# An encoder trunk on one core: the attention's first loads, the decays' sums and the experts' weight splits at other places

## What is computed

```python
h = rmsnorm(x, g_mix)
q, k, v, z, xbc, dtf, dtb, ga, gs = split(h @ w_in)
ya = windowed_gqa(q, k, v, sink, bias) @ w_attn_out
ys = ssd_branch(z, xbc, dtf, dtb, ...) @ w_ssd_out
x = x + (sigmoid(ga) * ya + sigmoid(gs) * ys) @ w_out
x = x + hier_moe(rmsnorm(x, g_ffn), router_g, router_e, w_gate_up, w_down)
x = x + sigmoid(rmsnorm(x, g_ple) @ w_ple_gate) * (p @ w_ple_proj)
return rmsnorm(x, g_final)
```

## Time and profile before

| what | us |
|---|---|
| three runs | 1834.16, 1846.12, 1836.23 |
| median | 1836.23 |
| the profiled execution, by the device | 1842.91 |
| its span, first to last instruction | 1840.8 |
| PE busy in the span | 1726.6 |

### The profile page before, as it was taken

How to read it: one execution, slowest core, us unless ns; L and a number is a source line. 1 busy time by engine, 2 the same in 40 slices (tenths; PEclk the granted TensorE clock), 3 DMA queues, 4 the chain that set the end, 5 groups by cost and what they waited for, 6 DMA issues and landing times. The chain is left out here.

```text
span 1840.8 us, 27069 instructions
## 1 busy us (share of the span) xinstructions
PE 1726.6 (94%) x10450; PEld 1417.9 (77%) x10451; DVE 885.6 (48%) x1027; ACT 597.5 (32%) x1010; POOL 414.3 (23%) x278
## 2 busy tenths in 40 slices
PE   6999999899999989999999999997999987998897
PEld 5878888787877757777888888885788876785786
DVE  5201777202034127742688425323757886940674
ACT  4311222231111126643455324112534433442332
POOL 3011111111111101002100022000356556652330
PEclk8999999999999999999899999998999998998899
DMA  5211222323355322017675344224767775742452
GB/s 196 86 63 58 78 77 77 110 75 112 129 180 186 89 72 64 27 41 223 221 193 155 127 139 149 80 70 164 259 213 275 282 296 199 282 176 105 163 194 92
DMA packets 115836, 265.90 MB, mean 144 GB/s; under 512 B 13011, under 2 KB 59555, under 8 KB 115740
## 3 DMA queue, kind: packets, MB, share of 16 engines
q1 hardware_dynamic: 99484, 209.11, 34.8%
q0 software_dynamic: 8320, 30.43, 4.9%
q10 hardware_dynamic: 7936, 25.01, 3.8%
HBM read 192.95 MB, written 71.55 MB: 144 GB/s over the span
## 5 line engine op out<-in xcount | busy, mean ns | idle before, releaser
L2139 DVE TENSOR_TENSOR ex_wlo<-ex_raw,ex_whi 128x1024 fp32r<-128x1024 f32 x102 | 166.8, 1649 | 6.9 <-ACT ex_whi L2133 6.9
L2135 DVE CAST ex_whi<-ex_raw 128x1024 fp32r<-128x1024 f32 x96 | 95.2, 997 | 71.0 <-DMA ex_raw<-experts 67.4
L2716 PE MATMUL rt_p<-ex_whi,ex_xh 128*128 x280 | 115.6, 413 | 14.1 <-issue 7.5
L286 PE MATMUL rest_p<-hi_h,whi_in 128*128 128x512 f32 (+1 forms) x480 | 121.9, 362 | 0.0
L286 PE MATMUL rest_p<-lo_h,whi_in 128*128 128x512 f32 (+1 forms) x480 | 119.9, 358 | 0.0
L286 PE MATMUL rest_p<-hi_h,wlo_in 128*128 128x512 f32 (+1 forms) x480 | 119.6, 357 | 0.0
L2717 PE MATMUL rt_p<-ex_wlo,ex_xh 128*128 x280 | 111.3, 397 | 0.0
L2718 PE MATMUL rt_p<-ex_whi,ex_xl 128*128 x280 | 111.3, 397 | 0.0
L889 ACT ACTIVATE rest_out<-rest_p 128x1024 f32<-128x1024 f32 x20 | 20.5, 1025 | 248.0 <-PE rest_p L286 248.0
L286 PEld LDWEIGHTS rest_p<-hi_h,whi_in 128*128 128x128 f32 x480 | 80.1, 188 | 22.1 <-issue 8.2
L920 POOL TENSOR_TENSOR wlo_in<-wraw_in,whi_in 128x1024 fp32r<-128x1024 f32 x18 | 43.8, 2434 | 230.5 <-ACT whi_in L883 230.5
(11 more groups left out here) (393 smaller groups left out, 4072.0 us busy)
## 6 DMA issues: line engine op xcount, KB each, us to landing
ex_raw<-experts SPq DMA_DIRECT2D x96, 512.0 KB, 6.1
wraw_in<-units SPq DMA_DIRECT2D x36, 512.0 KB, 4.4
y_slots<-ex_y ACTq DMA_DIRECT2D x35, 512.0 KB
rest<-rest_out SPq DMA_DIRECT2D x20, 640.0 KB, 6.0
scan_e<-erow SPq DMA_DIRECT2D x32, 256.0 KB
xtok<-conv_tok SPq DMA_DIRECT2D x10, 640.0 KB, 3.3
z_x<-x SPq DMA_DIRECT2D x10, 512.0 KB, 4.0
ao_gate<-rest SPq DMA_DIRECT2D x8, 640.0 KB, 5.1
```

The source lines that it names most:

```text
L286: mm = pe.matmul(out[:, n, 0:size], w[:, kk, :], h[:, kk, c:c + size], start=(kk == 0 and w is whi and h is hi), stop=(kk == ktiles - 1 an ...
L2135: eng.tensor_copy(self.hi[:, e % 2, n, :], self.raw[e % 2][:, n, :]).then_inc(self.w_hi[n], 1)
L2139: eng.tensor_tensor(self.lo[:, e % 2, n, :], self.raw[e % 2][:, n, :], self.hi[:, e % 2, n, :].bitcast(F32), ALU.subtract).then_inc(self.w ...
L2716: pe.matmul(gu[s][:, :], xh[s][:, kk, :], hi, start=(kk == 0), stop=False)
```

## The change

Three edits.

1. The loads of the first two query blocks and key windows, of V and of the sink move from the attention into the stage in front. A new class `Windows` holds these tiles and their semaphores. In the projection SP loads the sink before its loop and, at c = 18, waits for the states' last store, for earlier stores, for the stores of tiles 0 to 5 and for POOL's memset of the key windows, then issues the five loads ahead of store 18; at the stage's end it waits for them. The memset stands at the end of POOL's stream in that stage. The attention keeps the loads for n from 2, has no warm-up, and doesn't wait for V, the sink or the first windows.
2. In PE's order of the projection, product 1 comes ahead of the sums, and the rows' groups follow products 2 and 3; the bias line stands right behind the third group.
3. In the experts DVE does hi(n), lo(n), and then waits for its own low part before the next unit.

```diff
--- before.py
+++ after.py
@@ -815,7 +815,32 @@
         dve.memset(bias[:, 2, :, 2 * P:], NEG)
-def stage_project_rest(k, ctx, block, hi, lo, q, ring, xt_stored, ch_stored, early_copied, early_stored, first_lo, tok_copied):
+class Windows:
+    def __init__(self, k):
+        self.k, o = k, O_R2 + 9 * 4096
+        self.q = k.at("q_blk", [P, 2, 4, P], F32, o)
+        self.k_win = k.at("k_win", [P, 2, BAND], F32, o + 4096)
+        self.v = k.at("v_ch", [P, T], F32, O_W + 6 * 4096)
+        self.sink = k.at("sink", [P, N_HEADS], F32, O_KEEP + 2304)
+        self.qk_in = k.sems(None, "qk_in0", "qk_in1")
+        self.v_in, self.k_zero, self.sink_in = k.sems(None, "att_v_in", "att_k_zero", "att_sink_in")
+    def table(self, n):
+        return 1 if n in (0, QB) else 2 if n in (QB - 1, NT - 1) else 0
+    def load(self, sp, n):
+        s, rest = n % 2, self.k.d["rest"]
+        sp.dma_start(self.q[:, s, :, :], rest[0:4 * P, n * P:(n + 1) * P].rearrange("(m p) t -> p m t", p=P)
+                     ).then_inc(self.qk_in[s], 16)
+        a = 1 if self.table(n) == 1 else 0
+        b = 2 if self.table(n) == 2 else 3
+        sp.dma_start(self.k_win[:, s, a * P:b * P], rest[4 * P:5 * P, (n - 1 + a) * P:(n - 1 + b) * P]
+                     ).then_inc(self.qk_in[s], 16)
+def stage_project_rest(k, ctx, block, hi, lo, q, win, ring, xt_stored, ch_stored, early_copied, early_stored, first_lo, tok_copied):
     nc, d = k.nc, k.d
@@ -856,6 +881,7 @@
                 load(2 + s, s)
             decays.sync(sp)
             tables.sync_tables(sp)
+            sp.dma_start(win.sink[:, :], d["sink"].partition_broadcast(P)).then_inc(win.sink_in, 16)
             for c in range(n_tiles):
                 if c + 4 < n_tiles:
                     load(c + 4, c % 2)
@@ -867,9 +893,23 @@
                     states.load(sp, 1)
                 if FIRST <= c < FIRST + states.STEPS - 2:
                     states.load(sp, c - FIRST + 2)
+                if c == n_tiles - 2:
+                    states.wait_stored(sp)
+                    sp.wait_ge(early_stored, 16 * EARLY)
+                    for s in range(2):
+                        sp.wait_ge(xt_stored[s], 96)
+                        sp.wait_ge(stored[s], 48)
+                    sp.wait_ge(win.k_zero, 1)
+                    for n in range(2):
+                        win.load(sp, n)
+                    sp.dma_start(win.v[:, :], d["rest"][5 * P:6 * P, :]).then_inc(win.v_in, 16)
                 store(c, c % 2)
             for s in range(2):
                 sp.wait_ge(stored[s], 16 * (n_tiles // 2 + 1))
+                sp.wait_ge(win.qk_in[s], 32)
+            sp.wait_ge(win.v_in, 16)
+            sp.wait_ge(win.sink_in, 16)
         @block.scalar
         def _(act):
@@ -927,6 +967,8 @@
             with pool.Fori(3, n_tiles // 2) as i:
                 for s in range(2):
                     rest(2 * i + s, s)
+            states.wait_stored(pool)
+            pool.memset(win.k_win[:, :, :], 0.0).then_inc(win.k_zero, 1)
         @block.vector
         def _(dve):
@@ -957,14 +999,14 @@
                                 wlo[:, s, :].rearrange("p (k c) -> p k c", k=KT), hi, lo, KT).then_inc(mm_done, 1)
             product(0, 0)
+            product(1, 1)
             pe.wait_ge(tok_copied, 33)
             decays.tensor(pe)
-            product(1, 1)
+            product(2, 0)
             decays.tensor_rows(pe, 0)
             decays.tensor_rows(pe, 1)
-            product(2, 0)
+            product(3, 1)
             decays.tensor_rows(pe, 2)
-            product(3, 1)
             tables.tensor_line(pe)
             product(4, 0)
             product(5, 1)
@@ -1204,7 +1246,7 @@
-def stage_attention(k, ctx, block, att_hi, att_lo, ring):
+def stage_attention(k, ctx, block, att_hi, att_lo, ring, win):
@@ -1214,13 +1256,11 @@
     UNITS = 2 * NT
     if True:
         o = O_R1 + 10 * 4096
...
         vn = k.at("v_tok", [P, NT + 4, N_KV, HEAD + 1], F32, o + 12288)
         pt = k.at("probs_t", [P, 4, BAND], F32, o + 19616)
...
         @block.sync
         def _(sp):
-            sp.wait_ge(v_zero, 1)
-            for n in range(NT):
-                s = n % 2
-                if n >= 2:
-                    sp.wait_ge(score_done, 2 * n - 2)
-                sp.dma_start(qs[:, s, :, :], d["rest"][0:4 * P, n * P:(n + 1) * P].rearrange("(m p) t -> p m t", p=P)
-                             ).then_inc(qk_in[s], 16)
-                a = 1 if table(n) == 1 else 0
-                b = 2 if table(n) == 2 else 3
-                sp.dma_start(ks[:, s, a * P:b * P], d["rest"][4 * P:5 * P, (n - 1 + a) * P:(n - 1 + b) * P]
-                             ).then_inc(qk_in[s], 16)
+            for n in range(2, NT):
+                sp.wait_ge(score_done, 2 * n - 2)
+                win.load(sp, n)
                 if n == 3:
                     for u in range(2):
                         sp.dma_start(next_raw[:, u, :], d["units"][U_AO + u]).then_inc(next_in, 16)
         @block.gpsimd
         def _(pool):
-            pool.memset(ks[:, :, :], 0.0).then_inc(v_zero, 1)
             pool.memset(vn[:, :, :, :], 0.0).then_inc(v_zero, 1)
-            pool.wait_ge(v_zero, 2)
+            pool.wait_ge(v_zero, 1)
             pool.memset(vn[:, :, :, HEAD:HEAD + 1], 1.0).then_inc(ones_set, 1)
             for s in range(2):
                 pool.wait_ge(next_in, 32)
@@ -1287,8 +1313,8 @@
         def _(pe):
             def score(u):
                 n, h, s = u // 2, u % 2, u // 2 % 2
-                if h == 0:
-                    pe.wait_ge(qk_in[s], 32 * (n // 2) + 32)
+                if h == 0 and n >= 2:
+                    pe.wait_ge(qk_in[s], 32 * (n // 2))
                 if u:
                     pe.wait_ge(scored, u)
@@ -1328,9 +1354,7 @@
                     mm = pe.transpose(ap_[:, m, :], att[:, n % 2, m * P:(m + 1) * P], ident)
                 mm.then_inc(att_turned, 1)
-            warm_up(pe, k, pv_bank[:, :], 6)
             score(0)
-            pe.wait_ge(v_in, 16)
             for t in range(NT):
                 if t >= 2:
@@ -1359,8 +1383,6 @@
         @block.scalar
         def _(act):
-            act.dma_start(vt[:, :], d["rest"][5 * P:6 * P, :]).then_inc(v_in, 16)
-            act.dma_start(sink[:, :], d["sink"].partition_broadcast(P)).then_inc(sink_in, 16)
             act.preload_act_table(ACT.Exp)
             def exp(u, i):
@@ -1400,7 +1422,6 @@
         @block.vector
         def _(dve):
-            dve.wait_ge(sink_in, 16)
             dve.tensor_scalar(nsink[:, :], sink[:, :], -1.0, None, ALU.mult).then_inc(sink_neg, 1)
             dve.wait_ge(sink_neg, 1)
@@ -2649,15 +2670,15 @@
         def _(dve):
             dve.wait_ge(pp_done, NT)
             for e in range(1, N_EXP + 1):
-                ew.split_hi(dve, e, 0)
                 for n in range(6):
-                    if e == 1 and n == 3:
+                    if e == 1 and n == 4:
                         for s in range(2):
                             dve.wait_ge(pp_stored[s], 16 * (NT // 2))
-                    if n < 5:
-                        ew.split_hi(dve, e, n + 1)
+                    ew.split_hi(dve, e, n)
                     ew.split_lo(dve, e, n)
+                    dve.wait_ge(w_lo[n], e + 1)
         @block.gpsimd
         def _(pool):
...
```

More of the change, by code:

```diff
@@ L1216, in stage_attention @@
         o = O_R1 + 10 * 4096
-        qs = k.at("q_blk", [P, 2, 4, P], F32, o)
-        ks = k.at("k_win", [P, 2, BAND], F32, o + 4096)
-        vt = k.at("v_ch", [P, T], F32, o + 7168)
+        qs, ks, vt, sink, table = win.q, win.k_win, win.v, win.sink, win.table
+        win.qk_in = qk_in = k.sems(ctx, "att_qk_in0", "att_qk_in1")
         vn = k.at("v_tok", [P, NT + 4, N_KV, HEAD + 1], F32, o + 12288)
@@ L1222, in stage_attention @@
         att = k.at("att_tok", [P, 2, N_HEADS * HEAD], F32, o + 25760)
-        sink = k.at("sink", [P, N_HEADS], F32, o + 29856)
         nsink = k.at("nsink", [P, N_HEADS], F32, o + 29888)
@@ L1232, in stage_attention @@
         ap_ = ctx.enter_context(nc.psum_tensor("att_t", [P, 4, P], F32))
-        qk_in = k.sems(ctx, "qk_in0", "qk_in1")
-        names = ("v_in", "v_zero", "v_turned", "v_copied", "sink_in", "sink_neg", "score_done", "scored", "step",
+        names = ("v_zero", "v_turned", "v_copied", "sink_neg", "score_done", "scored", "step",
                  "probs", "turned", "pt_ready", "pv_done", "att_done", "att_turned", "att_hi_s",
                  "att_lo_s", "ready", "pv_step", "ones_set", "sunk")
-        (v_in, v_zero, v_turned, v_copied, sink_in, sink_neg, score_done, scored, step, probs,
+        (v_zero, v_turned, v_copied, sink_neg, score_done, scored, step, probs,
          turned, pt_ready, pv_done, att_done, att_turned, att_hi_s, att_lo_s, ready, pv_step, ones_set, sunk) = k.sems(
@@ L3046, in build @@
         q = SsdTiles(k)
+        win = Windows(k)
         with ExitStack() as ctx:
-            stage_project_rest(k, ctx, block, hi, lo, q, ring, *done)
```

(3 more changed lines are left out.)

2 lines of the change are left out of this document (removed).

## The result

The changed kernel takes 1824.59 us in the median of 13 runs (1820.5 to 1833.59), the kernel before, in 13 runs beside them, 1840.76 (1834.03 to 1848.44). The ratio is 0.9918, 95% interval 0.9899 to 0.9937: 0.8% faster. The forecast was 1824.5 and the range 1816 to 1834, but the agreement is closer than the single steps deserve: part of it is luck, as the sections behind show.

A forecast was written before the change was run, and what follows sets the result against it. PE bounds the kernel, busy 94% of 1840.8 us. Terms 4.5 + 3.6 + 11.5 = 19.6 take 1842.9 to 1823.3; the lowest timed run gives 1826.1; predicted the middle, 1824.5, range 1816 to 1834.

The forecast's parts named there:

- the accident: Experts, profiled execution: POOL's product for hidden values took 11.31 us, shut out by DVE's unbroken splits; PE waited 8.87.
- one of the signs of being wrong: Experts: the prediction is wrong if PE's waits for the low parts rise well above 4.1 us.
- First attention loads: Attention's start: early loads, no filler, score(0) right after the barrier; gain 4.5 us, bounds −2 to 8.1.
- rival 1: Attention without filler stays at half clock through its first units; its gain becomes 0 or −1, total 1829.5 us; chance 0.15.
- Sums a product later: Projection: PE's 5.04 us wait on DVE's decays goes, gain 6.8, less 3.2 exposed; net 3.6 us (1.6 to 4.4).
- The new wait: Projection: line product behind the third rows group waits 2.4 us for ACT's six copies; 0.8 more charged for the clock.
- Splits one by one: Experts: waits between DVE's splits let POOL in; net gain 11.5 us (−21 to 13).
- rival 2: Experts: POOL isn't let in, waits too short or its stall needs another cause; 1834.8 us; chance 0.13.
- the cover: Experts: DVE's 67.4 us idle for late weights hides the added 21.1 us (96 units × 0.22).
- rival 3: Experts: DVE becomes the bound; if none of its added 21.1 us is hidden, 1844.4 us; chance 0.05.
- The level: Whole kernel: timed runs some 11 us apart, as if one of three had the accident; the middle, 1824.5 us, predicted.

The follow-up runs named there:

- the old order and the wait: Changed kernel with hi(n+1) again issued ahead of lo(n), DVE's wait on its own low part kept behind each unit; ratio to the kernel before 0.9894.
- the gap behind every third unit: Changed kernel with hi(n+1) issued ahead of lo(n), DVE's wait on its own low part only behind every third unit; ratio to the kernel before 0.9912.

## Why the prediction was right, and where it was not

The waits and the filler that were to go went, and the sum came near (19.6 forecast against the profiled execution, 17.55 measured). But the three terms were mis-sized and their errors cancel in part, the reason that I gave for the accident is only part of it, and one of the signs of being wrong that I had named came: PE's waits for low parts rose well above 4.1 us.

**First attention loads.** The working by steps held: loads issued before store 18, score(0) at half clock, the softmax of unit 0 not late. I allowed 4.3 or 5.8 and took 4.5; it was 6.6. The step that failed is the time until the transposes end: I had them slow to 4.0 us, but they keep ACT's rhythm, 664.14 to 667.57, 3.4 us, and score(1), which I had taken nearer half clock (1.3 of the 2.1 us), was at full (in the run of the first edit alone it was not, 2.65 us). What I had put as rival 1 is real in small: without the filler the attention lost 1.4 of the 6.6 us later. The mean clock in windows of the changed kernel, then of the run with the old order and the wait (columns as in the earlier trace rows):

```profile
661.20:664.20 3.00, 2.92 (x9) 1.34 (x9) 1.59 (x1) 1.28 (x1) 1.77 (x2) 0.50 0.03 8
664.20:667.60 3.40, 2.59 (x13) 1.36 (x12) 3.24 (x2) 1.90 (x9) 0.00 (x0) 0.89 0.01 2
694.00:698.00 4.00, 2.59 (x24) 2.29 (x24) 3.25 (x5) 3.46 (x8) 2.23 (x1) 1.00 0.37 115
698.00:703.50 5.50, 5.50 (x32) 4.16 (x30) 1.85 (x4) 3.09 (x7) 0.00 (x0) 0.69 0.00 0
```

```profile
698.00:702.00 4.00, 4.00 (x21) 3.88 (x20) 1.37 (x4) 1.55 (x4) 0.00 (x0) 0.50 0.00 0
...
790.00:810.00 20.00, 18.36 (x98) 16.26 (x96) 7.00 (x14) 7.37 (x17) 0.00 (x0) 0.74 0.19 68
```

PE waits 1.41 us on the softmax at 695.7, and behind it the clock falls. With fillers, ahead of or behind the meeting, the attention took 127.7 to 128.5 us in seven profiles; in the six without it took 127.9, 128.2, 129.7, 129.9, 130.1 and 136.0. Why the clock falls in some of them and not in others, these runs do not show.

**Sums a product later.** I forecast 3.6; the projection became 5.0 us shorter in the pair of profiles, 3.4 with that edit alone. The new wait is 2.25 or 2.26 us in all seven profiles that have it (2.4 forecast: no row had the 0.35 of semaphore and start, and it measured 0.19, 2.25 less the copies' 2.06). What comes behind the wait differs from one execution to the next; the changed kernel, the second edit alone and the gap behind every third unit:

```profile
406.40:413.40 7.00, 7.00 (x34) 5.44 (x33) 0.68 (x1) 2.25 (x3) 2.83 (x3) 1.00 0.48 88
```

```profile
408.80:412.20 3.40, 3.40 (x11) 2.71 (x11) 0.63 (x1) 1.19 (x3) 0.73 (x1) 0.50 0.74 128
```

```profile
406.40:413.40 7.00, 6.97 (x17) 4.39 (x17) 0.68 (x1) 2.24 (x3) 1.87 (x3) 0.51 0.42 73
```

With the clock at full behind the wait, in three profiles, the projection took 313.2 us; with a fall as in the second, in three, 314.7 or 314.8; with the long one 316.4. So the clock cost nothing, 1.6 or 3.2 us, 1.1 in the mean of the seven, where I had charged 0.8. The term was about right, and the profile of the changed kernel was lucky in it. With the line product a product later the wait is gone and the projection takes 311.1, so its price was exposed, as put.

**Splits one by one.** I forecast 11.5; the experts became 9.0 us shorter. With gaps, of which 0.03 us is one, the accident did not come in nine executions, so the first half of rival 2, that the waits are too short, falls. Its second half, that POOL's stall needs another cause besides, stands: an unbroken series of DVE is not enough for it, as the last section shows.

The step that failed is the cover, "DVE stood idle for late weights for 67.4 us before its casts, three times the price, so that hides it". That is a sum over the stage. PE's waits for low parts rose from 4.1 to 10.2 us where I had charged 0.7 and credited 0.7: 7.4 of them stand between 1495 and 1545 us, where experts have few blocks and DVE has no idle time, and 2.8 at four places before that. So rival 3 holds in part, at some 5 us (9.8 in the mean of the kernels with two gaps, 4.8 of those with none) instead of 21.1. Not all of that is the gaps themselves: the longest wait, 2.70 us, ends with a subtraction that took 3.57 us beside a product of POOL.

The waits on POOL's hidden values fell by 9.1 and those on low parts rose by 6.1, 3.0 of gain. Most of the rest is the clock. The whole stage, before and changed (columns as in the earlier trace rows):

```profile
1320.80:1688.10 367.30, 340.92 (x1594) 277.21 (x1594) 242.56 (x192) 143.51 (x243) 208.36 (x137) 0.97 0.63 227
```

```profile
1311.50:1669.50 358.00, 335.93 (x1594) 273.34 (x1594) 258.15 (x192) 143.73 (x243) 201.71 (x137) 0.99 0.65 233
```

The same 1594 matmuls kept PE busy for 5.0 us less, at a mean granted clock of 0.99 and not 0.97; its idle time fell by 4.3. Of the 5.0, 2.6 behind the accident were foreseen. The first 46 us of the stage are another part (before, then changed):

```profile
1320.00:1366.00 46.00, 42.03 (x189) 34.20 (x190) 33.21 (x24) 18.55 (x30) 26.85 (x20) 0.93 0.56 189
```

```profile
1311.00:1356.00 45.00, 40.61 (x194) 33.19 (x195) 33.32 (x24) 18.55 (x30) 29.05 (x20) 1.00 0.58 203
```

This part is not the edit's: in the same 46 us the clock was 0.96 with the third edit alone and 0.93 with the filler put back, and both have the edit. It is luck of the two profiled executions, and what sets it these runs do not show.

**The level.** I took one timed run of three to have the accident. With more runs of before, its median was 1840.76, and three of four profiled executions without a gap had it. What the third edit is worth in the mean is some 6 us by the run of it alone (0.33%) and some 7.5 by the run in which it is undone (0.9959 against 0.9918), not the 11.5 that I drew from one profile.

## What to carry to other kernels

A long instruction on one engine where its like are short is worth a look at what the neighbouring engine does meanwhile; where an unbroken series stands there, one wait that it needs anyway, as a subtraction on the cast just issued, can let the other in. A second lengthens the chain: here it added some 4 us of PE's waits, which the timed runs could not tell. An engine's idle time is cover only in the stretch where it stands, so a price per unit is weighed against the stretch with the least of it. Filler products that warm PE up cost little where they run while the engines wait for each other (0.6 us here), and much behind that: taking out the 8.16 us of them brought the first turn 6.6 us forward. Where the clock falls in one execution and not in the next, one pair of profiles says little about a term of a microsecond or two.

## What the runs showed that I had not expected

POOL and DVE excluded one another for very different lengths. At 1517.25 a subtraction on DVE took 3.60 us instead of 1.22 while POOL's product of 2.40 us ran; there DVE waited out one instruction. At 1516.51, with the third edit undone, POOL waited out a whole series on DVE, 9.5 us. The Trainium skill, SBUF — State Buffer, section "Who interferes with whom", gives the pair of ports to whoever issues first for the whole instruction. The first case agrees on the whole instruction (3.60 is 1.22 and 2.38), but not on who is first: by the rows DVE starts 0.11 us ahead of POOL's 1517.36. The second goes beyond it, since POOL waited for many instructions and not for one.

That the series had no gaps does not explain this alone. All three accidents struck the same hidden product, the 20th of 35. In the kernel before, 51 of POOL's two-operand instructions in this stage start beside a DVE instruction whose successor overlaps it, and 50 of them took at most 1.1 us more than the shortest of their kind: POOL got in behind one DVE instruction at the latest. With the second edit alone, also without gaps, the 20th got in. Its rows, and then what DVE did in the kernel before in front of the accident of the earlier trace rows:

```profile
1519.26 0.90 POOL L2676 TENSOR_TENSOR ex_hid<-ex_up,ex_silu 128x256 f32<-128x256 f32 x1 [5.99 <-ACT ex_up L2771]
```

```profile
1517.22 2.35 DVE L2139 TENSOR_TENSOR ex_wlo<-ex_raw,ex_whi 128x1024 fp32r<-128x1024 f32 x2
1519.49 1.83 DVE L2135 CAST ex_whi<-ex_raw 128x1024 fp32r<-128x1024 f32 x2
```

```profile
1519.46 2.35 DVE L2139 TENSOR_TENSOR ex_wlo<-ex_raw,ex_whi 128x1024 fp32r<-128x1024 f32 x2
```

In both POOL's product starts some 0.3 us before a subtraction ends, with two casts next on DVE. In one the casts wait (1.83 us, not 1.28) and POOL takes 0.90; in the other the casts go on and POOL takes 11.31. What decides this is open. What the runs show is that a product once shut out stayed so until the series ended, and that no product was shut out where there were gaps.

The clock behind a wait of PE was not the same in each execution. Behind the line product's wait of 2.25 us it stayed full in three profiles and fell in four. Behind the meeting, six fillers with 1.71 us of idle time left score(0) at 1.56 us in two profiles, and five with 1.98 us left it at 2.52 in one; whether the filler, the idle time or chance made that difference these runs do not show.
